# A hybrid encoder layer on one core: decay exponents by running sums and VectorE differences instead of TensorE matmuls

## The reference

```python
def hgrn2_chunk(S, q, k, v, logf):
    b = jnp.cumsum(logf, axis=1)
    inter = jnp.einsum('blhk,bhkv->blhv', q * jnp.exp(b), S)
    diff = b[:, :, None] - b[:, None, :]
    dec = jnp.exp(jnp.where(causal[None, :, :, None, None], diff, -jnp.inf))
    A = jnp.einsum('blhk,bmhk,blmhk->bhlm', q, k, dec)
    intra = jnp.einsum('bhlm,bmhv->blhv', A, v)
    bl = b[:, -1]
    k_dec = k * jnp.exp(bl[:, None] - b)
    S_new = jnp.exp(bl)[..., None] * S + jnp.einsum('blhk,blhv->bhkv', k_dec, v)
```

## Time and profile before

| | |
|---|---|
| time, median of 3 runs | 1229.45 us (1228.81 to 1230.55) |
| the profiled execution: its own time | 1232.34 us |
| its span in the profile | 1230.6 us |
| PE busy / DVE busy / ACT busy over the span | 89% / 58% / 49% |
| mean granted clock of TensorE | 0.947 of full speed |

### The profile page before, as it was taken

The page is one execution under the profiler, slowest core; times in us unless marked ns, Lnnn a source line. Parts: engine busy times, 40 slices in busy tenths (PEclk is TensorE's granted clock), DMA queues, the critical chain, the costliest instruction groups (busy, mean ns, idle before and its releaser), DMA issues. The chain is left out here.

```text
span 1230.6 us, 26353 instructions
## 1 busy us (share of the span) xinstructions
PE 1095.6 (89%) x8820; PEld 898.8 (73%) x8821; DVE 708.4 (58%) x1321; ACT 602.1 (49%) x1226; POOL 107.1 (9%) x237
## 2 busy tenths in 40 slices
PE   4789999999999999999949999549999998999936
PEld 3688788977898778977837878337877776777722
DVE  3623555245632565326645665777886674767538
ACT  5634445334553444534453212156876664767433
POOL 0000000000000000000000011120011001100150
PEclk9799999999999999999969999659999999999978
DMA  8632222141222321223226341369999996999565
GB/s 308 226 92 74 80 83 60 36 141 53 67 70 58 95 79 35 65 74 118 83 69 212 103 155 60 127 207 338 394 388 351 319 332 229 365 311 350 188 246 205
DMA packets 202399, 210.53 MB, mean 171 GB/s; under 512 B 15612, under 2 KB 169076, under 8 KB 202036
## 3 DMA queue, kind: packets, MB, share of 16 engines
q1 hardware_dynamic: 183120, 177.25, 43.4%
q0 software_dynamic: 5712, 18.23, 4.1%
q10 hardware_dynamic: 13492, 13.96, 3.2%
HBM read 185.32 MB, written 24.08 MB: 170 GB/s over the span
## 5 line engine op out<-in xcount | busy, mean ns | idle before, releaser
L2019 DVE TENSOR_TENSOR experts_w_lo<-all_raw_more,experts_w_hi 128x2048 fp32r<-128x2048 f32 x48 | 108.4, 2287 | 7.2 <-ACT experts_w_hi L1900 7.2
L2019 DVE TENSOR_TENSOR experts_w_lo<-all_raw,experts_w_hi 128x2048 fp32r<-128x2048 f32 x48 | 109.6, 2284 | 4.9 <-ACT experts_w_hi L1900 4.9
L923 PE MATMUL early_ps_proj<-early_w_hi,early_h_hi 128*128 128x512 f32 x256 | 106.4, 416 | 2.6 <-ACT mixers_decay L756 2.6
L2187 PE MATMUL experts_ps_g<-experts_w_hi,experts_x_hi 128*128 128x512 f32 x256 | 104.5, 408 | 2.2 <-DVE experts_x_lo L2025 2.2
L925 PE MATMUL early_ps_proj<-early_w_hi,early_h_lo 128*128 128x512 f32 x256 | 101.2, 395 | 0.0
L2189 PE MATMUL experts_ps_g<-experts_w_hi,experts_x_lo 128*128 128x512 f32 x256 | 100.9, 394 | 0.0
L924 PE MATMUL early_ps_proj<-early_w_lo,early_h_hi 128*128 128x512 f32 x256 | 100.6, 393 | 0.0
L2188 PE MATMUL experts_ps_g<-experts_w_lo,experts_x_hi 128*128 128x512 f32 x256 | 100.5, 393 | 0.0
L1196 DVE TENSOR_TENSOR mixers_qd_t<-mixers_turned,early_tables 128x128 f32<-128x128 f32 (+1 forms) x36 | 10.1, 281 | 152.7 <-ACT mixers_turned L804 135.4
L1900 ACT ACTIVATE experts_w_hi<-all_raw 128x2048 fp32r<-128x2048 f32 x48 | 91.5, 1911 | 5.2 <-DMA all_raw<-in_W_up_e_dram 4.7
L1900 ACT ACTIVATE experts_w_hi<-all_raw_more 128x2048 fp32r<-128x2048 f32 x48 | 91.6, 1913 | 2.0 <-DMA all_raw_more<-in_W_up_e_dram 1.4
(11 more groups left out here) (358 smaller groups left out, 2687.9 us busy)
## 6 DMA issues: line engine op xcount, KB each, us to landing
all_raw_more<-in_W_down_e_dram SPq DMA_DIRECT2D x128, 256.0 KB, 5.4
all_raw<-in_W_gate_e_dram SPq DMA_DIRECT2D x96, 256.0 KB, 5.4
all_raw<-in_W_up_e_dram SPq DMA_DIRECT2D x96, 256.0 KB, 6.5
all_raw<-in_W_in_dram SPq DMA_DIRECT2D x32, 512.0 KB, 4.9
all_raw<-in_W_ada_dram SPq DMA_DIRECT2D x32, 512.0 KB, 4.7
condition_w_ada_in<-in_W_ada_dram SPq DMA_DIRECT2D x4, 2048.0 KB, 12.7
all_raw_more<-in_W_gate_e_dram SPq DMA_DIRECT2D x32, 256.0 KB, 7.2
all_raw_more<-in_W_up_e_dram SPq DMA_DIRECT2D x32, 256.0 KB, 7.3
```

Source lines behind the costliest of these rows:

```text
L923: pe.matmul(out, xhi, whi, start=(k == 0), stop=False)
L2019: dve.tensor_tensor(w_lo[:, 2 * p:2 * p + 2], raw_pair[p], f32(w_hi[:, 2 * p:2 * p + 2]), ALU.subtract).then_inc(lo_done, 1)
L2187: pe.matmul(out, x_hi[:, k, :], w_hi[:, c, at], start=(k == 0), stop=False)
```

## The change

TensorE no longer makes exponents. DVE replaces `log_f` in place by its running sum, tile by tile, once per round (`run`, nine scans, behind a new wait for ACT's logarithm). For each step it subtracts: eight differences of 128 x 128 from the running sum and one of its columns, spread over the frames (`spans`), then one operation that clears the sign bits of seven of the eight tables, read as integers (`sizes`). ACT's `decays` reads the running sum and these tables from SBUF, two exponentials in place of three, the second with scale -1. `spans(i+1)` and `sizes(i+1)` stand in DVE's queue behind rotary(i). Gone are `turn_log`, `log_high`, `log_low`, `exponents`, the table `steps`, its transfer and its copy, and some waits for them on PE: project(1, 0) no longer waits for the exponentials of tile 0, and scores no longer for those of the next tile.

```diff
                 def decays(i):
                     w = frames(i)
                     act.wait_ge(d_done, n[9] + (i + 1))
                     act.wait_ge(kl_done, n[9] + i)
                     act.wait_ge(ql_done, n[9] + i)
-                    act.activation(decay[:, 8, 0:w], ps_cum[:, 0:w], ACT.Exp)
-                    act.activation(decay[:, 4:8, 0:w], ps_d[:, :, 0:w], ACT.Exp)
-                    front = ps_p[(i + 1) % 2].rearrange("p (c l) -> p c l", l=P)
-                    for lo, hi in [(0, 4)] if w == P else [(0, 1), (3, 4)]:
-                        last = act.activation(decay[:, lo:hi, 0:w], front[:, lo:hi, 0:w], ACT.Exp)
+                    act.activation(decay[:, 8, 0:w], log_f[:, at(i):at(i) + w], ACT.Exp)
+                    for lo, hi in [(0, 8)] if w == P else [(0, 1), (3, 8)]:
+                        last = act.activation(decay[:, lo:hi, 0:w], span[:, lo:hi, 0:w], ACT.Exp, scale=-1.0)
                     last.then_inc(exp_done, 1)
...
-                    if i + 1 < NT:
-                        log_high(i + 1)
...
-                            pe.wait_ge(exp_done, n[9] + 1)
...
-                        if k == 7 and i + 1 < NT:
-                            turn_log(i + 1)
...
-                def turn_log(i):
...
-                def exponents(i):
...
-                    pe.wait_ge(exp_done, n[9] + min(i + 2, NT))
...
                     if i == 0:
                         project_sample()
-                    if i == 0 or 1 < i < NT:
-                        exponents(i)
-                    if i == 0:
-                        turn_log(1)
-                    elif i < NT:
+                    if 0 < i < NT:
                         project(i, 0)
-                    if i == 1:
-                        exponents(1)
...
-            dve.wait_ge(fetched, 16)
-            dve.tensor_copy(steps[:, :, :], decay[:, :, :]).then_inc(cleared, 1)
+            dve.wait_ge(cleared, 1)
...
+                def run(i):
+
+                    f = log_f[:, at(i):at(i) + frames(i)]
+                    dve.tensor_tensor_scan(f, s.const("ones", 0, frames(i)), f, 0.0, ALU.mult, ALU.add)\
+                       .then_inc(sum_done, 1)
+
+                def spans(i):
 
                     w = frames(i)
-                    dve.wait_ge(lfh_done, n[9] + (i + 1))
-                    dve.tensor_tensor(lf_lo[0:w, :], ps_tr[0:w, 3, :], f32(lf_hi[0:w, :]), ALU.subtract)\
-                       .then_inc(lfl_done, 1)
+                    dve.wait_ge(sum_done, n[9] + (i + 1))
+                    dve.wait_ge(exp_done, n[9] + i)
+                    b = log_f[:, at(i):at(i) + w]
+                    dve.tensor_tensor(span[:, 0, 0:w], b, b[:, w - 1:w].broadcast_to([P, w]), ALU.subtract)
+                    for c, h in enumerate(LEVELS, 1):
+                        if 2 * h > w:
+                            continue
+                        pairs = b.rearrange("p (b l) -> p b l", l=2 * h)
+                        last = dve.tensor_tensor(span[:, c, 0:w].rearrange("p (b l) -> p b l", l=2 * h), pairs,
+                                                 pairs[:, :, h - 1:h].broadcast_to([P, w // (2 * h), 2 * h]), ALU.subtract)
+                    last.then_inc(level_done, 1)
+
+                def sizes(i):
+
+                    w = frames(i)
+                    dve.wait_ge(level_done, n[9] + (i + 1))
+                    lo = 1 if w == P else 3
+                    size = span[:, lo:8, 0:w].bitcast(I32)
+                    dve.tensor_scalar(size, size, 0x7FFFFFFF, None, ALU.bitwise_and).then_inc(d_done, 1)
...
-                log_low(0)
+                dve.wait_ge(logf_done, n[1] + 1)
+                for i in range(NT):
+                    run(i)
+                spans(0)
+                sizes(0)
...
-                    if i + 1 < NT:
-                        log_low(i + 1)
                     if 0 < i < NT:
                         rotary(i)
+                    if i + 1 < NT:
+                        spans(i + 1)
+                        sizes(i + 1)
```

More of the change, by code:

```diff
@@ L73 @@
               k_decay=2 * HEADS, s_decay=2 * HEADS)
-LATE = dict(steps=(len(LEVELS) + 2) * P)
-CONSTS = {**KEPT, **TABLES, **LATE}
+CONSTS = {**KEPT, **TABLES}
 N_KEPT, N_TABLES = sum(KEPT.values()), sum(TABLES.values())
-AT = {name: at for part in (KEPT, TABLES, LATE) for name, at in zip(part, np.cumsum([0, *part.values()]).tolist())}
+AT = {name: at for part in (KEPT, TABLES) for name, at in zip(part, np.cumsum([0, *part.values()]).tolist())}
 def width(i):
@@ L109, in constants @@
     c["own_block"] = m // 32 == l // 32
-    between = lambda ref: ((m > ref) & (m <= l)) | ((m > l) & (m <= ref))
-    c["steps"] = np.stack([m > l, *(between(l // (2 * h) * (2 * h) + h - 1) for h in LEVELS), m <= l], 1)
     c["iota"] = np.broadcast_to(np.arange(NE), (P, NE))
@@ L491, in phase_mixers @@
         gate = sb("gate", [P, 2, NTOK])
-        steps = sb("steps", [P, 9, P], F32R)
-        lf_hi = sb("lf_hi", [P, P], F32R)
-        lf_lo = sb("lf_lo", [P, P], F32R)
+        span = sb("span", [P, 8, P])
         decay = sb("decay", [P, 9, P])
@@ L538, in phase_mixers @@
         tr_done, qkt_done, qd_done = sem("tr_done"), sem("qkt_done"), sem("qd_done")
-        lft_done, lfh_done, lfl_done, d_done, exp_done = (sem("lft_done"), sem("lfh_done"), sem("lfl_done"),
-                                                          sem("d_done"), sem("exp_done"))
+        sum_done, level_done, d_done, exp_done = (sem("sum_done"), sem("level_done"), sem("d_done"),
+                                                  sem("exp_done"))
         summed = sem("summed")
@@ L554, in phase_mixers @@
                   f_done, logf_done, roped, rot_done, v_done, kdec_done, tr_done, qkt_done, qd_done,
-                  lft_done, lfh_done, lfl_done, d_done, exp_done, summed, ql_done, kl_done, lv_done, ra_done, masked_done,
+                  sum_done, level_done, d_done, exp_done, summed, ql_done, kl_done, lv_done, ra_done, masked_done,
                   ah_done, ahc_done, ar_done, o_done, s_done, ms_done, seed_log, seed_done, norm_step,
@@ L665, in _ @@
             late_stores(R - 1)
-            sp.wait_ge(fetched, 16 * 7)
+            sp.wait_ge(fetched, 16 * 6)
         @block.gpsimd
@@ L729, in read_block @@
                                 act.wait_ge(lv_done, n[9])
+                                act.wait_ge(exp_done, n[9])
                             act.activation(log_f[:, some_frames], src, ACT.Sigmoid)
@@ L770, in _ @@
                 act.activation(log_f[:, :], log_f[:, :], ACT.Ln).then_inc(logf_done, 1)
-                log_high(0)
                 read_block(3)
@@ L938, in project_sample @@
                     last.then_inc(proj_done, 1)
-                def turn_log(i):
-                    w = frames(i)
-                    if i == 0:
-                        pe.wait_ge(logf_done, n[1] + 1)
-                    pe.wait_ge(lfl_done, n[9] + i)
-                    pe.wait_ge(ar_done, n[9] + max(i - 1, 0))
-                    pe.transpose(ps_tr[0:w, 3, :], log_f[:, at(i):at(i) + w], ident).then_inc(lft_done, 1)
-                def exponents(i):
-                    w = frames(i)
-                    pe.wait_ge(lfl_done, n[9] + (i + 1))
-                    pe.wait_ge(exp_done, n[9] + i)
-                    pe.wait_ge(v_done, n[9] + i)
-                    pe.wait_ge(masked_done, n[9] + max(i - 1, 0))
-                    pe.wait_ge(ahc_done, n[8] + max(i - 2, 0))
-                    if i == 0:
-                        pe.wait_ge(t_read, n[12] + 12)
-                        pe.wait_ge(cleared, 2)
-                    front = ps_p[(i + 1) % 2].rearrange("p (c l) -> p c l", l=P)
-                    parts = [(ps_cum[:, 0:w], steps[0:w, 8, 0:w]), (ps_d[:, :, 0:w], steps[0:w, 4:8, 0:w])]
-                    parts += [(front[:, lo:hi, 0:w], steps[0:w, lo:hi, 0:w])
-                              for lo, hi in ([(0, 4)] if w == P else [(0, 1), (3, 4)])]
-                    for out, table in parts:
-                        pe.matmul(out, lf_hi[0:w, :], table, start=True, stop=False)
-                        last = pe.matmul(out, lf_lo[0:w, :], table, start=False, stop=True)
-                    last.then_inc(d_done, 1)
                 def scores(i):
@@ L1058, in _ @@
                 for p in range(3, 12):
-                    if p == 11:
-                        turn_log(0)
                     turned_piece(p // 3, p % 3, n[8] + (p // 3 + 1), (t_read, n[12] + (p - 2)))
@@ L1079, in _ @@
                     if i >= NT:
-                        next_piece(i - NT + 1, (exp_done, n[9] + 9))
+                        next_piece(i - NT + 1, (v_done, n[9] + 9))
                     if i >= 2:
```

11 lines of the change are left out of this document (1 added, 10 removed).

## The result

The changed kernel takes **1241.53 us** (median of 5 runs, 1238.15 to 1244.32) against 1230.55 for the kernel before in the same series: ratio **1.0081**, 95% interval 1.0055 to 1.0107. It is slower by 0.8%, where I had forecast 1226 with a range to 1240. A second series gave 1237.25 (12 runs), ratio 1.0050 (1.0034 to 1.0066), so the loss is real and its size is 6 to 11 us. The profiled execution after has a span of 1241.1 us.

What follows compares the result with a forecast made beforehand. PE was taken to bound the mixers' steps (busy 96.6 of 100 us). From 1232.3, -13 for the steps and +9.5 for clock falls gave 1228.8, 3.5 below; 1229.45 - 3.5 = 1226 us, range 1213 to 1240.

Steps and rivals of the forecast that it cites:

- The loop: Ordinary mixer step: DVE and ACT, one after the other, replace PE as bound, 10.34 us against 10.19 or 10.20.
- my sum: Added times for each kind of mixer step, clock held: -3.2 us per round, -13 us in all.
- R: Moment in a mixer step at which DVE would start rotary, 4.46 us after Q without log_low.
- Q: Moment in each mixer step when DVE starts scored(i-1), ending a wait for ACT's copies; 10.19 or 10.20 us apart in ordinary steps.
- the four steps that were to lose 0.15 each: Per round, three ordinary mixer steps and the one with an extra DVE instruction: +0.15 us each, +0.6.
- DVE's terms: New DVE work per mixer step: eight differences 1.74 us, wait for its own last one 0.03, sign operation 0.66.
- the rival of one per cycle: DVE's sign operation takes 1.08 us: +9.5 us in all, 1235 with falls of the clock; chance 0.14.
- A third of them, 8 falls of 1.2, +9.5 us: TensorE's clock falls in a third of 24 new pauses in the mixers' steps, each fall costing 1.2 us.
- 24 places: New PE pauses, six a round, behind scores without `condition` and ahead of the first project(1, 1), where the clock may fall.
- Rival 2: TensorE's clock low in nearly every mixer step, deciding from about eleven falls of 1.2 us: 1245 to 1254; chance 0.12.
- nothing in the phases behind starts on its own time: Argument against a later phase swallowing the mixers' shift by waiting for something else (1229 us, chance 0.04).
- The second look at POOL: POOL beside DVE's sign operation: a block would move POOL's result from R + 4.5 to R + 4.9, sum unchanged.

Runs made afterwards that it cites:

- fill_three: Changed kernel plus six unused 512-column matmuls behind the scores in steps 1, 4 and 8 of a round: 1223.17 us, ratio 0.9925.
- after_again: The changed kernel once more, unchanged: 1237.25 us, ratio 1.0050 to the kernel before.
- after: The changed kernel against the kernel before, first series: 1241.53 us, ratio 1.0081.
- no_sign_fill: Changed kernel, sign operation replaced by a one-element copy, exponential's scale -0.001, six extra matmuls in steps 1, 4, 8: round 137.02 us.
- early_spans: Changed kernel with spans and sizes worked out one step earlier into a second buffer: 1218.65 us, ratio 0.9904.
- before_again: The kernel before once more, unchanged: 1230.79 us in one execution.
- fill_all: Changed kernel plus six unused matmuls behind the scores in steps 1, 3, 4, 6, 7 and 8: 1221.71 us, ratio 0.9932.
- fill_other: Changed kernel plus six unused matmuls only in steps 3, 6 and 7, pauses 1.5 to 1.7 us: 1237.02 us, ratio 1.0049.
- work_first_before: Kernel before, with useful work put ahead of the waits on TensorE, ScalarE and VectorE: 1279.38 us, ratio 1.0385.
- before: The kernel without the change, exponents on TensorE: 1230.55 us.
- fill_two: Changed kernel plus two unused matmuls instead of six in steps 1, 4 and 8: 1238.71 us, ratio 1.0060.
- work_first: Changed kernel with scores and projection ahead of waiting transposes, ScalarE's copy ahead of exponentials, VectorE's gate behind keys: 1171.91 us, ratio 0.9516.
- work_first_early_spans: Changed kernel with useful work ahead of the waits and spans worked out one step earlier: 1170.28 us, ratio 0.9502.
- no_spans: Changed kernel, differences and sign operation replaced by one-element copies, span tile 1.0, exponential's scale -0.001: round 139.85 us.
- early_spans_fill: Changed kernel with spans one step earlier and six unused matmuls in steps 1, 4 and 8: 1216.11 us, ratio 0.9882.
- early_spans_fill_348: Changed kernel with spans one step earlier and six unused matmuls in steps 3, 4 and 8: 1210.20 us, ratio 0.9815.

## Why the prediction was wrong

- **The loop: right.** With the clock held (fill_three), the steps came out as in my sum: 11.00 for the one with the transfers (11.01), 10.35 for the `condition` step (10.42), 10.23 and 10.24 for ordinary ones (10.34). A round, from the second to the third, is 3.27 us shorter than before; the sum had 3.2. Rows of the changed kernel, in the step with the extra DVE instruction:

```profile
306.89 0.42 DVE L1191 TENSOR_TENSOR mixers_qk_cos<-mixers_qkv,early_tables 128x256 f32<-128x256 f32 x1
...
310.49 0.31 ACT L739 ACTIVATE mixers_decay<-mixers_log_f 128x128 f32<-128x128 f32 x1 [0.33 <-DVE mixers_span L1081]
```

  R is 4.65 behind Q (4.66 in that step of the kernel before), ACT's decays R + 3.60 (3.67 in the sum) with DVE's span as the releaser, the next Q 2.18 behind (2.21). A little luck is in the total: of the four steps that were to lose 0.15 each, three lost 0.02 to 0.05 and the seventh 0.35, which I can't explain. And the sum did not say what the kernel without the new work showed, that an ordinary step could not have gone below some 10.0 in this order.
- **DVE's terms: right.** Groups of the changed kernel by line:

```profile
L1071 DVE TENSOR_TENSOR mixers_span<-mixers_log_f 128x128 f32<-128x128 f32 x224 | 47.9, 284 | 0.0
L1081 DVE TENSOR_SCALAR mixers_span<-mixers_span 128x896 int32<-128x896 int32 x32 | 20.1, 627 | 1.1
L1066 DVE TENSOR_TENSOR mixers_span<-mixers_log_f 128x128 f32<-128x128 f32 x32 | 9.0, 283 | 0.0
```

  A difference takes 0.28 and starts 0.20 behind the last; the sign operation takes 0.627 for 896 integers, at the rate of the copy and the scaled forms (0.63 by their rows; 1.08 at half of it), so the rival of one per cycle is out. The Trainium skill (VectorE: DVE Perf Modes, section The perf-mode tier table) leaves integers out; this row adds them at the fast rate.
- **"A third of them, 8 falls of 1.2, +9.5 us": this term failed.** Right were the mechanism, the pause and the low level's matmuls of 0.63. But the falls are 11, and not spread by chance over 24 places: they sit in the three steps of a round whose pause is 2.3 us or more, and hardly one such pause goes without. And each costs more: fill_three against after_again saves 12.47 - 11.04 = 1.43 in the first step, 11.90 - 10.35 = 1.55 and 11.06 - 9.99 = 1.07 in the others, and 0.5 at the end of the round, 4.53 in all. Over the four rounds, the last of which has only two falls, it is 16 us and not 9.5. 1229.45 - 13 + 16 = 1232.5, against 1237 and 1241 measured, so the sign of the change turns on this term. Rival 2 said that the sign turns "from about eleven falls of 1.2 us on"; eleven came, at 1.5 each. Rival 2's own case, a low clock in nearly every step at 1245 to 1254, did not.
- The pauses were in my sum step by step, as PE's wait for normalise and copies. I gave all 24 places the same chance in place of listing their lengths. That a length of 2.3 us is on the bad side and 1.7 mostly on the good one, no row that I had could tell; it came with these runs.
- **The rest, 5 to 9 us, I had let be nothing.** Part of it is the slow issues of transfers: after has two and after_again one, and after takes 2.0 us longer from the first Q to the last. Part lies outside the mixers ("nothing in the phases behind starts on its own time"); some of that is shown below.
- **The second look at POOL: a block does occur, and leaves the sum as it was.** In the changed kernel the first of POOL's four instructions takes 0.27 in such a step and ends 0.05 behind the end of the sign operation:

```profile
309.83 0.63 DVE L1081 TENSOR_SCALAR mixers_span<-mixers_span 128x896 int32<-128x896 int32 x1
...
310.24 0.27 POOL L680 TENSOR_TENSOR mixers_norm<-mixers_norm 128x2 f32<-128x2 f32 x1 [9.81 <-ACT mixers_mean_sq L771]
```

  Without the sign operation (no_sign_fill) it takes 0.20. POOL's result is there in time for ACT even so; in early_spans, where the block is 0.3 longer, it is not.

## What to carry to other kernels

Work taken off the bounding engine turns into pauses of that engine unless its order of instructions lets it run on; before counting the gain, list the new pauses by place and length, since here the few long ones (2.3 us and more) brought a low clock over the dense work behind them. Ask too what a step would take with that work gone and nothing put in its place: here 10.0 against 10.2, so the ordinary steps had almost nothing to win. When a change frees an engine, look next for work whose operands are ready and put it ahead of the wait (here 65 us, against 14 for matmuls without use). And judge such a change together with the order that it permits: the same edit cost 6 to 11 us in one order and gained 107 in another, or 60 against the old kernel in the old order.

## What the hardware showed beside this

**A gather issued by GpSimd waits for a VectorE operation that started 0.05 us earlier.** At the entry to the experts POOL issues a gather while DVE begins two differences of 2048 columns. Timelines of POOL and DVE, changed kernel (after_again):

```profile
815.05 3.12 POOL L1815 DMA_INDIRECT experts_x_rows<-h_scratch,experts_index  x1 [0.27 <-POOL experts_index L1811]
```

```profile
815.00 2.29 DVE L1986 TENSOR_TENSOR experts_w_lo<-all_raw,experts_w_hi 128x2048 fp32r<-128x2048 f32 x1 [4.91 <-ACT experts_w_hi L1867]
```

The kernel before (before_again):

```profile
808.36 1.01 POOL L1848 DMA_INDIRECT experts_x_rows<-h_scratch,experts_index  x1 [0.27 <-POOL experts_index L1844]
```

```profile
808.36 4.53 DVE L2019 TENSOR_TENSOR experts_w_lo<-all_raw,experts_w_hi 128x2048 fp32r<-128x2048 f32 x2 [4.90 <-ACT experts_w_hi L1900]
```

fill_all, where the gather starts 0.12 ahead of DVE:

```profile
796.59 1.00 POOL L1824 DMA_INDIRECT experts_x_rows<-h_scratch,experts_index  x1 [0.27 <-POOL experts_index L1820]
```

```profile
796.71 4.49 DVE L1995 TENSOR_TENSOR experts_w_lo<-all_raw,experts_w_hi 128x2048 fp32r<-128x2048 f32 x2 [4.91 <-ACT experts_w_hi L1876]
```

Where DVE starts 0.05 to 0.07 us ahead, the gather takes 3.1 and ends some 0.9 behind the end of DVE's first difference (after, after_again, fill_other, early_spans, work_first_before); where DVE starts at most 0.02 ahead, or behind, the gather takes 1.0 (before, before_again, fill_all, fill_three, fill_two, work_first, work_first_early_spans, no_sign_fill, no_spans). early_spans_fill lies between, 0.04 to 0.05 ahead, with 1.0. In early_spans_fill_348 DVE is 2.6 us ahead, so the gather (788.68, 2.77) starts inside the second difference, and it too ends 0.9 behind that one's end:

```profile
786.07 4.49 DVE L1995 TENSOR_TENSOR experts_w_lo<-all_raw,experts_w_hi 128x2048 fp32r<-128x2048 f32 x2 [4.91 <-ACT experts_w_hi L1876]
```

The Trainium skill (SBUF - State Buffer, section SBUF: two separate sides) says that a DVE operation in a two-port mode, or one with two SBUF inputs against a GpSimd one that reads SBUF, and a GpSimd one hold the shared port in turn, for the whole instruction, whichever comes first. The rows agree as far as DVE comes first, and so does POOL's 0.52 beside the sign operation above. They don't agree where the gather comes first: DVE's two differences take 4.49 us in fill_all, beside the gather, as they do in early_spans_fill_348, where no gather runs beside the first.

The blocked gather is 2.1 us of what the changed kernel loses there. Behind it stands a pause of PE of 1.67 us ahead of its second matmul (L2155, released by "issue") that the kernel before hasn't. All six changed kernels without extra matmuls have it, at 1.4 to 1.9 us, three of them with a gather of 1.0, so it does not come from the gather; where it comes from is open. Both profiles of the kernel before and both of the changed one fell the same way with the gather; whether that is the rule of the two kernels or chance, two of each don't tell. From the first Q to the last the two changed profiles lose 4.8 and 6.8 us against the kernel before, and they reach the first Q 1.2 to 2.8 us earlier; the rest of the 6 to 11 us lies behind the mixers and is explained in part only.

**More work on an engine can shorten a kernel.** 72 to 144 matmuls whose result nobody reads saved 14 to 16 us.
